# Fillers that shift where the operands of some matrix products begin in on-chip memory

## The reference

```python
# first block
z = rmsnorm(x) @ w_in                       # q, k, v, gates, convolution inputs
mixed = concat(3 dilated window attentions (mixed by softmax of their lse) * silu(gate), gated conv)
x = x + rmsnorm(mixed @ w_out)              # first output projection  ("o1")
# second block
p = rmsnorm(x) @ w_in_2
y = g_a * (rmsnorm(mLSTM(q, k, v, i, f)) * sigmoid(o)) + g_b * spatial_gating(u, sv)
x = x + y @ w_out_2                         # second output projection ("o2")
x = x + softmax(q k^T / 16) v @ w_xo_2      # attention to 256 memory rows; third projection ("o3")
# 32 experts in 4 groups, 2 experts of one group for each token
x = x + sum_k gate_k * ((silu(xn @ w1[e_k]) * (xn @ w3[e_k])) @ w2[e_k])
out = rmsnorm(x)
```

## Time and profile before

| | us |
|---|---|
| median of 3 runs | 2654.49 (2652.89 to 2657.09) |
| the profiled execution | 2656.93 |
| its span, first to last instruction | 2655.10 |
| o1, o2, o3 on TensorE, first to last MATMUL | 597 to 691, 1540 to 1637, 1856 to 1962 |
| blocks of the experts on TensorE | 2003 to 2611 |
| sum and norm at the end | 2611 to 2655 |

### The profile page before, as it was taken

One profiled execution on the slowest core, in us unless ns is written; L12 is line 12 of the kernel. 1 busy time (PEld: TensorE's weight loads), 2 busy tenths in 40 slices (PEclk: granted clock), 3 DMA queues, 4 the chain that ended last, 5 costly groups with the idle time before them and its releaser, 6 DMA issues. The chain is left out here.

```text
span 2655.1 us, 30070 instructions
## 1 busy us (share of the span) xinstructions
PE 2502.4 (94%) x11958; PEld 2004.0 (75%) x11958; DVE 1255.3 (47%) x1583; ACT 1142.3 (43%) x1612; POOL 596.3 (22%) x497
## 2 busy tenths in 40 slices
PE   8999998889999999999999999998978999999992
PEld 6888874448787888878887877885866888888882
DVE  6420315554303112126443943014138888888886
ACT  4212225553341222124232732244225777777773
POOL 1312302213131222233121741254101111111100
PEclk9999999999999999999999999999988999999996
DMA  4313121203310031233225633351546999999995
GB/s 174 107 64 92 54 82 40 80 13 132 111 64 32 32 130 46 72 108 105 90 68 203 238 135 111 103 183 45 177 174 242 376 380 377 388 381 373 374 363 232
DMA packets 146581, 434.78 MB, mean 164 GB/s; under 512 B 16232, under 2 KB 66632, under 8 KB 133768
## 3 DMA queue, kind: packets, MB, share of 16 engines
q1 hardware_dynamic: 95536, 374.23, 37.5%
q10 hardware_dynamic: 38120, 31.50, 3.6%
q0 software_dynamic: 12784, 27.11, 2.9%
HBM read 377.70 MB, written 72.91 MB: 170 GB/s over the span
## 5 line engine op out<-in xcount | busy, mean ns | idle before, releaser
L2795 DVE TENSOR_TENSOR ex_w_lo<-ex_w,ex_w_hi 128x2048 fp32r<-128x2048 f32 x198 | 448.0, 2290 | 73.3 <-ACT ex_w_hi L2734 71.4
L2734 ACT ACTIVATE ex_w_hi<-ex_w 128x2048 fp32r<-128x2048 f32 x198 | 378.9, 1915 | 21.6 <-PE ex_pb L2665 14.5
L220 POOL TENSOR_TENSOR p_w_lo<-w_raw,p_w_hi 128x512 fp32r<-128x512 f32 (+1 forms) x146 | 191.3, 1343 | 624.7 <-ACT p_w_hi L248 593.2
L220 POOL TENSOR_TENSOR p_w_lo_rest<-w_raw,p_w_hi_rest 128x512 fp32r<-128x512 f32 x88 | 118.0, 1373 | 255.9 <-ACT p_w_hi_rest L248 255.9
L845 DVE CUSTOM_DVE_ANT_0 att_sc<-att_ps_s,logc 128x128 f32<-128x128 f32 (+7 forms) x96 | 71.7, 752 | 120.8 <-PE att_ps_s L780 120.4
L273 PE MATMUL p_ps<-p_w_hi,hT_hi 128*128 128x512 f32 (+1 forms) x320 | 120.7, 377 | 0.0
L275 PE MATMUL p_ps<-p_w_hi,hT_lo 128*128 128x512 f32 (+1 forms) x320 | 118.3, 370 | 0.0
L274 PE MATMUL p_ps<-p_w_lo,hT_hi 128*128 128x512 f32 (+1 forms) x320 | 118.0, 369 | 0.0
L248 ACT ACTIVATE p_w_hi<-w_raw 128x512 fp32r<-128x512 f32 (+1 forms) x133 | 74.6, 599 | 91.2 <-PE mix_ps_rest L275 49.3
L2434 POOL DMA_INDIRECT ex_x<-xn_rows,slot_token x33 | 34.2, 1036 | 346.4 <-PE ex_px L2639 323.9
L273 PE MATMUL ex_py<-ex_w_hi,ex_hT_hi 128*128 128x512 f32 x264 | 107.3, 407 | 1.9 <-DVE ex_hT_lo L2804 1.9
(11 more groups left out here) (507 smaller groups left out, 6260.4 us busy)
## 6 DMA issues: line engine op xcount, KB each, us to landing
ex_w<-w SPq DMA_DIRECT2D x99, 2048.0 KB, 13.8
w_raw<-w_in SPq DMA_DIRECT2D x42, 1024.0 KB, 5.1
w_raw<-w_out SPq DMA_DIRECT2D x8, 1024.0 KB, 8.0
x_rows<-o_x SPq DMA_DIRECT2D x16, 512.0 KB, 2.6
qk_columns<-ml_qk_first ACTq DMA_DIRECT2D x16, 512.0 KB, 3.2
w_raw<-w_xkv SPq DMA_DIRECT2D x8, 1024.0 KB, 6.2
plain_cols<-x SPq DMA_DIRECT2D x8, 512.0 KB, 8.3
w_raw<-w_in SPq DMA_DIRECT2D x16, 256.0 KB, 3.9
```

The costliest lines, as they stand in the source:

```text
L220: emit(self.lo(n)[:, 0:w], self.half(n // (KC // 2), w)[:, n % (KC // 2), :], self.hi(n)[:, 0:w].bitcast(F32), ALU.subtract).then_inc(self ...
L2734: nc.scalar.activation(w_hi[:, n % RING, :], raw_half(n), ACT.Copy).then_inc(hi_done, 1)
L2795: nc.vector.tensor_tensor(w_lo[:, n % RING, :], raw_half(n), w_hi[:, n % RING, :].bitcast(F32), ALU.subtract).then_inc(down_lo if m == "w2 ...
```

## The change

Two fillers are allocated on the right stack, behind `ml_decays` (384 bytes) and behind `rt_w` (384 bytes). Two small buffers on the left grow: `rt_bias` from 256 to 512 bytes, `ex_idx` from 128 to 512 bytes. No instruction is added, taken away or moved on any engine: both programs have the same 17352 instructions in the same order with the same waits, and outside of the fillers all buffers have their old size.

```diff
+LINE = 128
@@ experts
-        idx = sb("idx", [P, ALIGN], I32)
+        idx = sb("idx", [P, LINE], I32)
@@ build
                     decay = rows.enter_context(nc.sbuf_tensor("ml_decays", [P, MH, NT], F32, side="right"))
+                    rows.enter_context(nc.sbuf_tensor("ml_decays_rest", [P, LINE - MH * NT], F32, side="right"))
@@ build
-                bias = late.enter_context(nc.sbuf_tensor("rt_bias", [P, 2 * ALIGN], F32))[:, 0:NG + NE]
+                bias = late.enter_context(nc.sbuf_tensor("rt_bias", [P, LINE], F32))[:, 0:NG + NE]
                 logits = late.enter_context(nc.psum_tensor("rt_scores", [P, NT, 64], F32))
                 wr = front.enter_context(nc.sbuf_tensor("rt_w", [P, KC, NG + NE], F32, side="right"))
+                front.enter_context(nc.sbuf_tensor("rt_w_rest", [P, LINE - KC * (NG + NE) % LINE], F32, side="right"))
```

## The result

Six runs of the changed kernel have a median of 2639.40 us (2633.82 to 2640.11), six runs of the kernel before on the same chip 2654.76 us (2652.89 to 2657.09). The ratio is 0.9934 with an interval of [0.9924, 0.9945]: 0.66% faster. Predicted were 2639.6 us. The profiled execution of the changed kernel took 2638.07 us with a span of 2636.3; that of before took 2656.93 with 2655.1.

The account below looks back on a forecast made before the run. TensorE was taken to set the pace, with transfers close behind. Terms 1.6 + 2.2 + 12.1 - 1.0 = 14.9 us gave 2642.0 us against the profiled execution, 2639.6 against the median; the 8-in-10 range was 2634 to 2651 us.

Parts of the forecast that it names:

- What bounds it: Whole kernel: TensorE sets the pace, busy 2502 of 2655 us, with transfers not far behind in the experts.
- That starts set the pace: On TensorE, the same MATMUL takes 390 ns where all operands begin at 384, 397 ns at other starts.
- o2, 1.6 us: Second output projection: 8 tiles at 11.80 us for 12.02 give 1.8 us, cut to 1.6 for the first tile.
- o3, 2.2 us: Third projection: 8 tiles at 11.80 us for 12.09 give 2.3 us, cut to 2.2 for the first tile.
- Experts, 12.1 us: Experts' stage: blocks fall from 18.11 to 17.72 us, 0.39 each over 31 blocks, a gain of 12.1 us.
- o1's pace: Tiles where all operands already begin at 384: 11.80 us each; an experts block equals one and a half such tiles.
- The check by the other view: Experts, by single durations: 72 MATMULs at 5 ns less make 0.36 us a block.
- 31 blocks: Experts: 31 of 33 blocks gain; the first ends in a wait, the last has 24 MATMULs at the low clock.
- The stall, -1.0 us: Experts: late landings in single heavy blocks stall TensorE, losing 1.0 us over the stage, bounds 0 and 12.1.
- That starts do not matter: Traffic beside the MATMULs makes the 5 to 7 ns, so no change, 2654.5 us; chance 0.09.
- Transfers as the bound: Experts: transfers cannot go below about 17.95 us a block, 2645.7 us, or 2650.7 if already at their limit; chance 0.11.
- the common start is bad for `up`: Experts' w3 MATMULs: equal starts put all 48 at 408 ns, making the kernel slower, 2664.7 us; chance 0.04.

Follow-up runs that it names:

- experts_only: Kernel before with only the two grown left buffers (`rt_bias`, `ex_idx`), without the right-stack fillers; 2642.62 us, ratio 0.9948.
- projections_only: Kernel before with only the two right-stack fillers, behind `ml_decays` and `rt_w`; 2653.19 us, ratio 0.9987.
- lo_apart: Changed kernel with a 256-byte filler ahead of `xT_lo` and `hT_lo`, so these begin 256 bytes off; 2638.96 us, once.
- apart_256_128: Changed kernel with the experts' stationary operands moved against the moving ones, xT by 256 bytes and hT by 128; 2645.68 us, once.
- fillers_128: Kernel before with 128-byte fillers behind `ml_decays` and `rt_w`, `ex_idx` grown to 256 bytes, `rt_bias` as before; 2639.15 us, ratio 0.9935.
- two_fewer: Changed kernel with 2 of each experts block's 72 MATMULs left out; 2624.39 us, once.
- apart_32_64: Changed kernel with the experts' stationary operands moved against the moving ones, xT by 32 bytes and hT by 64; 2653.10 us, once.
- moving_apart: Changed kernel with the experts' moving operand `w_lo` moved by 128 bytes, `w_hi` and the stationary operands unmoved; 2647.55 us, once.
- run 228: Not a run or kernel: "run" is a verb here, and 228 ns the first of seven listed distances in the trace of before.
- apart_4_16: Changed kernel with the experts' stationary operands moved against the moving ones, xT by 4 bytes and hT by 16; 2651.20 us, once.
- six_fewer: Changed kernel with 6 of each experts block's 72 MATMULs left out; 2615.22 us, once.

## Why the prediction was right

**What bounds it** held: TensorE, without a gap, before and after.

**That starts set the pace** held, and was shown and not only argued: each stack's fillers alone change the pace of their own stage and of nothing else (`experts_only`, `projections_only`), and moving the stationary operands by 4, 16, 32, 64 or 128 bytes, or one moving operand by 128, brings the slow pace back. The form of the rule was too strong: a common start modulo 512 is not needed, equal or 256 apart is enough (`lo_apart`, `apart_256_128`, `fillers_128`). Whether equality counts, or that each start is 128 modulo 256, is open.

**o2, 1.6 us**: measured 1.5 from its second tile on. **o3, 2.2 us**: 3.0 in the ledger. Between the first and the last group of transposes of o3 it is 86.61 against 84.83, 1.8 us; 0.5 are the pace of the two tiles ahead of them (24.02 against 23.48), which makes 2.3 of pace; and 0.7 are the clock of the last transposes. How much a single execution can add here shows in `experts_only`: with the tiles of before in o3 it has 110.65 against 112.18 in the same stretch, because the low clock at o3's start is missing: 22.49 us for these two tiles in place of 24.02. The stretch from 1852 to 1860 in before, the changed kernel and `experts_only`:

```profile
1852.00:1860.00 8.00, 5.58 (x14) 3.38 (x13) 1.30 (x3) 3.29 (x5) 2.38 (x1) 0.80 0.53 145
```

```profile
1852.00:1860.00 8.00, 5.79 (x18) 4.63 (x19) 1.30 (x3) 2.52 (x4) 2.37 (x1) 0.79 0.66 158
```

```profile
1852.00:1860.00 8.00, 5.58 (x19) 3.13 (x18) 1.30 (x3) 3.29 (x5) 1.75 (x1) 1.00 0.35 126
```

**Experts, 12.1 us**: 11.3. The mis-sized term is the block, 17.75 for 17.72, a gain of 0.36 for 0.39. The rest of o1's pace was all there; the switches to transposes and back cost 0.05 us above 1.5 tiles, which I had at 0.02 by an estimate. The check by the other view, 72 MATMULs at 5 ns, had the 0.36. I counted 31 blocks; of the 32 distances between blocks in the 11.3, 30 give 10.8 and the first two, which hold waits, 0.5. That the last block has 24 MATMULs at the low clock was a misreading: in the trace of before seven of them are at that clock and two more in part.

**The stall, -1.0 us**: measured 0. Single landings do come late, but the ring hides them: `two_fewer` shows 38 such waits in 400 us and TensorE still without idle time. Its cause was right in kind and too early in size: it begins between 17.30 us a block, where there is none, and 16.39, where there is 17.33 - 16.39 = 0.9 a block.

**Missed**: the clock, 1.6 us behind the last block's wait and 0.7 at o3's end. The faster pace was forecast at 1.6 + 2.2 + 12.1 = 15.9 and is 1.5 + 2.3 + 11.3 + 0.6 = 15.7 in the profile; with 2.3 of the clock and 0.8 of scatter this makes the 18.8. By the medians it is 15.4. That the sum of 14.9, with its stall of 1.0 that didn't come, lies within half a microsecond of this is luck. Single executions differ by more than the terms that went wrong, so the median says nothing on them.

**The rivals.** That starts do not matter is out. With it goes into doubt, for this stream, the sentence that the Trainium skill (TensorE: Matmul & The Clock Gate, Part 2) has on the loading of weights, that it "doesn't steal SBUF read bandwidth from the running matmul": distances of 227 ns with equal starts and 233 with others, at one clock and with the same instructions, say that where the operands begin costs time, and that the cost hangs on both (`apart_32_64` moves the stationary ones, `moving_apart` a moving one). That two reads meet is the plain explanation, but no run shows it: each MATMUL here has a weight load beside it. Transfers as the bound are out at 17.75, and where they become one in this kernel is now known. The figure of about 358 GB/s in the Trainium skill (SBUF — State Buffer, A bandwidth-pool intuition that's wrong) is half of what two cores share by that page's own working. It is no limit here, with one core at work: 396 GB/s over 400 us. That the common start is bad for `up` is out: `ex_pb`'s first kind fell from 408 to 401. Its reason was a misreading too. I took 408 and 391 for the two products that share a stationary operand. Single starts in the trace of before show another pattern: in `ex_pb` 238 and 229 ns take turns throughout, also among the four with `ex_xT_lo`, where no two share one, and in `ex_py` and `ex_pa` the distances run 228, 230, 233, 241, 232, 231, 232 with a period of seven, which fits neither the three kinds of `ex_py` nor the pairs of `ex_pa`. So what tells 408 from 391 is where the pattern stands, not which operand is used twice.

## What to carry to other kernels

When the same instruction from the same line has two durations in two stages at one clock and TensorE is gapless, compare where its operands begin: here stationary and moving starts that are equal modulo 256 bytes (both at 128 or 384) make 227 ns of a 128x512 product, and starts 4 to 128 bytes apart some 233. Look at distances between starts over whole periods, not at durations, since a mean of 391 may hide a neighbour's 408. Then ask what the faster engine must be fed with, and measure this by leaving work out: that gave the room (0.4 us a block) which no row of the kernel before did.

## What the runs showed of the hardware

- The distance between starts of consecutive 128x512 products (float32 in two parts, each with its own weight load) at a granted clock of 1.00: 227 ns for operands that begin 0 or 256 bytes apart modulo 512, at 128 or 384 (six kernels), means of 232 to 233 ns for 4, 16, 32, 64 and 128 apart. 4 bytes cost as much as 128.
- A mismatch is shared: with a third of the products mismatched, matched ones are late as well (`moving_apart`), and behind `ex_py` at 128 apart it takes eight matched products to come back to 227 (`apart_256_128`).
- Behind eight transposes the first product takes 318 ns and the next five 228 to 236, with equal starts and the identity at 128 or 384; then 227.
- The low clock behind the last block's wait of 1.90 us is there in five of the six profiled executions with blocks above 17.9 us (before, `projections_only`, `apart_256_128`, `moving_apart`, `apart_4_16`; not in `apart_32_64`), and in none of the eight with blocks of 17.75 or less. The stretch behind the last transposes is 33.4 to 33.7 us long in these five and 31.45 in six of the eight (less in the two that leave products out). What decides it has not been tried, nor whether it repeats within one kernel.
- Sustained transfers on one core: 396 GB/s over 400 us at a share of 0.97, in `two_fewer` and in `six_fewer`, where TensorE waits for them.

Open: whether it is equality that counts or 128 modulo 256 for each operand; whether the rule holds for other shapes, for 2-byte types, or where several products share one weight load. None of it was tried. Of the versions here that do the whole work none beats the changed kernel beyond the scatter; `fillers_128` equals it with less memory.
